# A two-block transformer kernel on one core: the opening rearranged (second row tile on ScalarE's DMA queue, first weight unit in two loads, row factors in fewer steps, meta tokens turned inside the first unit)

## The chip, the core and the metric

The kernel runs on one core of one Trainium2 chip. The core has a matrix engine (TensorE, PE in the rows), a vector engine (VectorE, DVE), an activation engine (ScalarE, ACT), a general engine (GpSimd, POOL) and a queue engine for transfers (SyncE, SP). ACT and POOL can issue transfers too. The five run their own instruction streams and meet at semaphores; each takes its instructions strictly in order, so one that waits holds up everything behind it on the same engine. The metric is the device time of one execution in microseconds (us). Matrices are float32, and each product is made from three passes over high and low parts, so weights are split before use: `whi` is the weight rounded to the matrix engine's format, `wlo` is the rest.

## The reference, cut to what matters

Two blocks follow each other on 256 rows of width 1024; 16 learned meta rows stand ahead of the real rows in the first block. What the change touches is only how the very first product is prepared:

```python
def rms_norm(x, g):
    xf = x.astype(jnp.float32)
    y = xf * lax.rsqrt(jnp.mean(xf * xf, axis=-1, keepdims=True) + RMS_EPS)
    return (y * g.astype(jnp.float32)).astype(x.dtype)

h = jnp.concatenate([filler, meta, x], axis=1)     # meta: 16 rows, x: 256 rows, width 1024
u = rms_norm(h, pre_mix_gain[l])
proj = u @ w_in[l]                                  # 1024 x 6656
# then: rope, windowed attention with meta keys, differential attention, gates,
# feed-forward, and the second block (delta rule, sparse attention, cross-attention,
# feed-forward); none of that is touched
```

## The kernel before

All weights stream through in units of 1 MB: a unit is 1024 rows by 256 columns (seen as 128 partitions x 8 x 256) or a shape of the same size. SP issues the loads into four buffers `raw`; ACT makes `whi` from `raw`, DVE makes `wlo`, each in halves (`split`), and PE multiplies. `plan` is a list of steps made by `schedule()`; each engine walks the same list and does its own part of each step, so the list fixes the order on every engine. The token `ahead` in the list lets the splits of coming halves stand early.

The opening before is this. SP loads row tile 0 of x, then row tile 1, then weight unit 0, a part of the constants (`ca`), unit 1 and so on; ACT issues the loads of the meta tokens (`metat`), of the identity matrix for transposes (`ca[:, 0:128]`) and of the gain columns (`pc[:, 0:8]`). The step `rows` computes for each of three row groups (tile 0, tile 1, meta) the sum of squares (ACT for tile 0 and meta, DVE for tile 1), the mean plus epsilon (DVE), the power -0.5 (POOL, `power`), and then the scaled rows `xs0` in halves of 512 columns: tile 0 and meta on DVE, tile 1 on ACT. The step `turn` transposes blocks of 128 columns by PE into PSUM and applies the gain: ACT writes the high part of the turned activations (`R1[0]`, "hi"), DVE the low part (`R1[1]`, "lo"). `turnm` does the same for the 16 meta rows, which become columns 256 to 271 of `R1`. The turned activations live in `R1b`.

Unit 0 is of the form `featk`: its split goes by halves of the contraction, so its first half (k-blocks 0 to 3) needs only lo 0 to 3 and the split (0, 0), and its second half needs lo 4 to 7 and (0, 1). It yields query columns, which the meta rows don't need. Unit 1 (keys) is the first that reads all 272 columns and so waits for the meta part, `norm_dve` key `("n1", "lo", 8)`.

Before PE's first real work it runs 13 matmuls on constants (`keep`), which depend on nothing but a memset.

## Time and profile before

| | |
|---|---|
| time, median of 3 runs | 960.5 us (960.37 to 960.55) |
| the profiled execution's own time | 960.5 us |
| its span, first to last instruction | 958.4 us |
| outside the span | 2.1 us |
| PE busy | 937.5 us, 98% |
| DVE, ACT, POOL busy | 674.6, 527.3, 137.9 us |
| granted TensorE clock, mean | 0.999 |
| first matmul of unit 0, of unit 1 | 12.82 us, 19.45 us |

Times inside the span are counted from its first instruction. Busy is the time in which an engine runs an instruction; waiting for a semaphore is not busy. A row of a timeline gives start, duration, engine, line, operation, what is written from what, and in brackets the idle time before it and who ended it. Successive instructions of one line and one pair of tiles are merged into one row with a count.

### The profile page before, as it was taken

What the parts mean: (1) busy time and instruction counts of PE and PEld (TensorE: products, weight loads), DVE (VectorE), ACT (ScalarE), POOL (GpSimd) and SP (SyncE); (2) the same over time, 40 slices, a digit from 0 to 9 for tenths busy, and PEclk for the clock granted to TensorE, in tenths of its full rate; (3) what the DMA queues carried; (4) which work ended last, traced back from release to release, by engine and by line L of the source; (5) the groups of instructions that cost most, each with busy time, mean ns of one, the idle gap of its engine ahead of it and who ended that gap; (6) DMA issues with size and microseconds to landing.
All of it is one profiled execution on the core that took longest, in us unless ns stands there. A gap on an engine that the chain in (4) does not pass through costs nothing.

```text
span 958.4 us, 15483 instructions
## 1 busy us (share of the span) xinstructions
PE 937.5 (98%) x6180; PEld 840.1 (88%) x6180; DVE 674.6 (70%) x1233; ACT 527.3 (55%) x1013; POOL 137.9 (14%) x159
## 2 busy tenths in 40 slices
PE   8999999999999999999999999899999999999996
PEld 7989888999999988888898899888798898888885
DVE  6888777777478676776758668767665567666765
ACT  6876665875456644444446686455454454344443
POOL 2211111220133000000001119941100000000001
PEclk9999999999999999999999999999999999999999
DMA  9544324343367555555565563300543455656441
GB/s 316 183 155 132 128 93 136 129 133 133 133 229 243 169 204 194 176 194 198 176 216 185 177 237 123 121 30 1 176 149 117 153 176 176 220 176 205 166 156 45
DMA packets 115863, 154.71 MB, mean 161 GB/s; under 512 B 2728, under 2 KB 98224, under 8 KB 115536
## 3 DMA queue, kind: packets, MB, share of 16 engines
q1 hardware_dynamic: 113376, 142.91, 44.9%
q0 software_dynamic: 1952, 10.42, 3.0%
q8 instruction: 49, 0.80, 0.4%
q10 hardware_dynamic: 464, 0.40, 0.2%
q14 instruction: 22, 0.18, 0.1%
HBM read 150.56 MB, written 3.16 MB: 160 GB/s over the span
## 4 chain that ended last, share of the span: by engine, by line
PE 89%; DVE 3%; POOL 3%; ACT 3%; issue 1%; DMA 0%; POOLq 0%; DVEq 0%; ACTq 0%
PE ps L847 14%; PE ps L823 8%; PE ps L825 8%; PE ps L824 8%; PE ps L848 7%; PE ps L1135 4%; PE ps L1108 4%; PE ps L1109 4%; PE ps L1110 4%; PE ps L866 4%; PE ps L868 4%; PE ps L867 4%; PE ps L809 3%; PE ps L836 2%; PE ps L838 2%; PE ps L837 2%
## 5 line engine op out<-in xcount | busy, mean ns | idle before, releaser
L1374 DVE TENSOR_TENSOR wlo<-raw,whi 128x1024 fp32r<-128x1024 f32 (+1 forms) x268 | 327.7, 1242 | 164.4 <-ACT whi L1986 164.0
L1986 ACT ACTIVATE whi<-raw 128x1024 fp32r<-128x1024 f32 (+1 forms) x268 | 273.8, 1050 | 129.9 <-PE ps L848 53.5
L847 PE MATMUL ps<-R1b,whi 128*128 128x512 f32 x576 | 201.8, 393 | 0.0
L823 PE MATMUL ps<-R1b,whi 128*128 128x256 f32 (+1 forms) x592 | 172.3, 291 | 0.8 <-DVE wlo L1374 0.8
L825 PE MATMUL ps<-R1b,wlo 128*128 128x256 f32 (+1 forms) x592 | 167.7, 283 | 0.0
L824 PE MATMUL ps<-R1b,whi 128*128 128x256 f32 (+1 forms) x592 | 167.5, 283 | 0.0
L848 PE MATMUL ps<-R1b,wlo 128*128 128x256 f32 x576 | 161.4, 280 | 0.0
L847 PEld LDWEIGHTS ps<-R1b,whi 128*128 128x128 f32 x576 | 108.1, 188 | 24.7 <-issue 0.5
L823 PEld LDWEIGHTS ps<-R1b,whi 128*128 128x128 f32 x592 | 111.6, 188 | 9.1 <-issue 7.9
L825 PEld LDWEIGHTS ps<-R1b,wlo 128*128 128x128 f32 x592 | 111.8, 189 | 0.0
L824 PEld LDWEIGHTS ps<-R1b,whi 128*128 128x128 f32 x592 | 111.5, 188 | 0.2
L848 PEld LDWEIGHTS ps<-R1b,wlo 128*128 128x128 f32 x576 | 108.2, 188 | 0.6
L2380 POOL TENSOR_TENSOR st<-st 128x1 f32<-128x1 f32 (+5 forms) x28 | 23.3, 838 | 375.4 <-DVE st L1367 299.8
L1108 PE MATMUL ps<-whi,R3ah 128*128 128x512 f32 x176 | 68.8, 391 | 0.0
L1109 PE MATMUL ps<-wlo,R3ah 128*128 128x512 f32 x176 | 68.8, 391 | 0.0
L1110 PE MATMUL ps<-whi,R3al 128*128 128x512 f32 x176 | 68.5, 389 | 0.0
L1986 ACT ACTIVATE F<-F 128x512 f32<-128x512 f32 (+6 forms) x58 | 28.9, 502 | 59.7 <-DVE F L1628 53.7
L1986 ACT ACTIVATE R3ah<-F 128x512 fp32r<-128x512 f32 x22 | 13.9, 632 | 68.1 <-DVE F L1650 68.1
L1617 DVE TENSOR_REDUCE F<-ps 128x256 f32<-128x512 f32 x72 | 49.3, 684 | 0.0
L1986 ACT ACTIVATE SC<-ps 128x512 f32<-128x512 f32 (+3 forms) x78 | 33.1, 429 | 21.0 <-PE ps L825 10.3
L1108 PEld LDWEIGHTS ps<-whi,R3ah 128*128 128x128 f32 x176 | 33.0, 188 | 7.2
L1110 PEld LDWEIGHTS ps<-whi,R3al 128*128 128x128 f32 x176 | 33.0, 188 | 7.2
(293 smaller groups left out, 1780.2 us busy)
## 6 DMA issues: line engine op xcount, KB each, us to landing
raw<-in_w_in SPq DMA_DIRECT2D x34, 1024.0 KB, 5.1
raw<-in_w_ffn_in SPq DMA_DIRECT2D x22, 1024.0 KB, 5.1
raw<-in_w_ffn_out SPq DMA_DIRECT2D x11, 1024.0 KB, 5.4
raw<-in_w_gate SPq DMA_DIRECT2D x11, 1024.0 KB, 5.3
raw<-in_w_up SPq DMA_DIRECT2D x11, 1024.0 KB, 5.3
raw<-in_w_down SPq DMA_DIRECT2D x11, 1024.0 KB, 6.0
raw<-in_w_out SPq DMA_DIRECT2D x8, 1024.0 KB, 5.1
raw<-in_w_xkv SPq DMA_DIRECT2D x8, 1024.0 KB, 5.5
```

What stands on the lines that cost most here:

```text
L823: e.matmul(o, hi[:, kt, c], R[0][:, kt, 0:n], start=kt == 0, stop=False)
L824: e.matmul(o, hi[:, kt, c], R[1][:, kt, 0:n], start=False, stop=False)
L825: m = e.matmul(o, lo[:, kt, c], R[0][:, kt, 0:n], start=False, stop=kt == 7)
L847: e.matmul(B[:, :].rearrange("p (a n) -> p a n", a=2), hi[:, kt, c], R[2][:, :, kt, 0:256], start=kt == 0, stop=False)
L848: m = e.matmul(B[:, 0:256], lo[:, kt, c], R[0][:, kt, 0:256], start=False, stop=kt == 7)
L866: e.matmul(B[:, 0:n], R[0][:, kt, c], hi[:, k, :], start=kt == 0, stop=False)
L1108: e.matmul(B[:, :], Fh[:, k, c], hi[:, k, d], start=j == 0 and k == 0, stop=False)
L1109: e.matmul(B[:, :], Fh[:, k, c], lo[:, k, d], start=False, stop=False)
L1110: m = e.matmul(B[:, :], Fl[:, k, c], hi[:, k, d], start=False, stop=end and k == 1)
L1374: e.tensor_tensor(half_of(wlo[i % HL], i, k), half_of(raw[i % RAW], i, k), f32(half_of(whi[i % HL], i, k)), SUB).then_inc(lo_split(i, (i, k)))
L1617: e.tensor_reduce(FSLOT[j % 2][0][:, at:at + 256], B[:, :].rearrange("p (a n) -> p n a", a=2), AX, ADD).then_inc(ffn_dve((kind, f, j, b)))
L1986: return e.activation(o, i, f, **kw)
```

## The change

Five edits, all in the opening:

1. Row tile 1 of x is loaded by ACT's queue, as its first transfer; the meta tokens become that queue's fourth and last.
2. Unit 0 of the weights is loaded in two transfers of 512 KB (k-blocks 0 to 3, then 4 to 7), with a semaphore of its own for the first.
3. Row factors: the mean plus epsilon is no longer a step of DVE. For tile 1 the DVE instruction that squares and sums takes the factor 1/1024 and starts from 1e-6; for tile 0 and meta POOL itself does that step ahead of its power. POOL runs one power on a constant before, at the start.
4. The scaling of tile 1's first half moves from ACT to DVE, that of the second half stays on ACT but stands behind the split (0, 0). Meta rows are scaled by POOL in one instruction of 16 x 1024.
5. The eight meta transposes of PE stand between the halves of unit 0; the gain step of DVE (`metax`) stands between lo 5 and lo 6, and the meta high and low parts (`metahl`) come behind the split (1, 0).

```diff
@@ schedule(): opening
         for j in range(2):
             take(0, j)
             step("ropek", j, 0)
+            if j == 0:
+                step("turnm")
-    step("rows", "n1")
+    step("first")
     ahead(1)
+    step("late")
     step("turn", "n1", (0, 2))
     ahead(2)
-    step("turn", "n1", (4, 6))
-    step("turnm")
+    step("turn", "n1", (4,))
+    step("metax")
+    step("turn", "n1", (6,))
+    ahead(3)
+    step("metahl")
@@ tensor: turnm
-                    p.wait_ge(norm_dve, ("n1", "sc", b // 4, 2))
+                    p.wait_ge(norm_pool, ("n1", "sc", 2))
@@ vector
+            def first():
+
+                v_, q = X[:, 1, :], stat(("n1", 1), 3)
+                d.wait_ge(*SOURCE["n1"][1])
+                ttr(xs0[1], v_, v_, 1.0 / 1024, 1e-6, MUL, ADD, q[:, 1:2]).then_inc(norm_dve(("n1", "ms", 1)))
+                for c, i in ((0, 0), (0, 1), (1, 0)):
+                    cs = slice(512 * c, 512 * c + 512)
+                    d.wait_ge(norm_pool, ("n1", "rs", i))
+                    ts(xs0[i][:, cs], X[:, i, cs], scale_of("n1", i)).then_inc(norm_dve(("n1", "sc", c, i)))
@@ scalar
             def split(i, k):
-                a.wait_ge(raw_in[i % RAW], i)
+                a.wait_ge(*((raw_first, 0) if (i, k) == (0, 0) else (raw_in[i % RAW], i)))
+            def first():
+                for i, (v_, m) in enumerate(rows_of("n1")):
+                    if i != 1:
+                        a.wait_ge(*SOURCE["n1"][i])
+                        act(xs0[i][0:m, :], v_, ACT.Square, accum_out=stat(("n1", i), 3)[0:m, 0:1]).then_inc(
+                            norm_act(("n1", "sq", i)))
+
+            def late():
+                a.wait_ge(norm_pool, ("n1", "rs", 1))
+                act(xs0[1][:, 512:1024], X[:, 1, 512:1024], scale=scale_of("n1", 1)).then_inc(norm_act(("n1", "sc", 1, 1)))
-            e.dma_start(metat, A["meta_tokens"]).then_inc(meta_in(0), 16)
+            e.dma_start(X[:, 1, :], A["x"].rearrange("a (t p) n -> p (a t) n", p=128)[:, 1, :]).then_inc(x1_in(0), 16)
             e.dma_start(ca[:, 0:128], A["const_a"][:, 0:128]).then_inc(id_in(0), 16)
             e.dma_start(pc[:, 0:8], A["params"][:, 0:8]).then_inc(mix_in(0), 16)
+            e.dma_start(metat, A["meta_tokens"]).then_inc(meta_in(0), 16)
@@ gpsimd
+            def first():
+                for i in (0, 1, 2):
+                    m = rows_of("n1")[i][1]
+                    q = stat(("n1", i), 3)[0:m]
+                    if i == 1:
+                        pool.wait_ge(norm_dve, ("n1", "ms", 1))
+                    else:
+                        pool.wait_ge(norm_act, ("n1", "sq", i))
+                        e.tensor_scalar(q[:, 1:2], q[:, 0:1], 1.0 / 1024, 1e-6, MUL, ADD).then_inc(norm_pool(("n1", "ms", i)))
+                        pool.wait_ge(norm_pool, ("n1", "ms", i))
+                    power(q[:, 2:3], q[:, 1:2]).then_inc(norm_pool(("n1", "rs", i)))
+                pool.wait_ge(norm_pool, ("n1", "rs", 2))
+                e.tensor_tensor(xs0[2][0:16, :], metat, scale_of("n1", 2).to_broadcast([16, 1024]), MUL).then_inc(
+                    norm_pool(("n1", "sc", 2)))
-            pool.wait_ge(set_dve, "half")
+            pool.wait_ge(set_dve, "one")
+            power(stat("warm", 1), ones).then_inc(set_pool("warm"))
@@ sync
-            e.dma_start(X[:, 1, :], x_src[:, 1, :]).then_inc(x1_in(0), 16)
...
+                dst = raw[i % RAW][:, 0:k * n].rearrange("p (k n) -> p k n", k=k)
+                if i == 0:
+                    e.dma_start(dst[:, 0:4, :], src[:, 0:4, :]).then_inc(raw_first(0), 16)
+                    src, dst = src[:, 4:8, :], dst[:, 4:8, :]
+                e.dma_start(dst, src).then_inc(raw_in[i % RAW](i), 16)
```

How the order stands on ACT from its first transfer to its first high parts of the turned activations, before; `in_x`, `in_meta`, `in_raw0` are the landings of row tile 0, of the meta tokens and of unit 0, and `in_raw_first` that of unit 0's first part:

```order
L2364 DMA F<-in_meta_tokens 16x1024
L2365 DMA ca<-in_const_a 128x128
L2366 DMA pc<-in_params 128x8
L1986 ACT_TABLE_LOAD
L1986 ACTIVATE F,st<-X 128x1024 [waits in_x]
L1986 ACTIVATE F,st<-F 16x1024 [waits in_meta]
L1986 ACTIVATE F<-X,st 128x512 [waits norm_pool]
L1986 ACTIVATE F<-X,st 128x512
L1986 ACTIVATE whi<-raw 128x1024 [waits in_raw0]
L1986 ACTIVATE R1b<-ps,pc 128x256 [waits norm_pe,in_mix]
```

And now, on the same engine:

```order
L2393 DMA X<-in_x 128x1024
L2394 DMA ca<-in_const_a 128x128
L2395 DMA pc<-in_params 128x8
L2396 DMA F<-in_meta_tokens 16x1024
L2004 ACT_TABLE_LOAD
L2004 ACTIVATE F,st<-X 128x1024 [waits in_x]
L2004 ACTIVATE F,st<-F 16x1024 [waits in_meta]
L2004 ACTIVATE whi<-raw 128x1024 [waits in_raw_first]
L2004 ACTIVATE F<-X,st 128x512 [waits norm_pool]
L2004 ACTIVATE R1b<-ps,pc 128x256 [waits norm_pe,in_mix]
```

The instruction that waits for the meta tokens still stands second, while their transfer has moved from the first place of the queue to the last; the first split has moved up by two places.

On POOL, from its last memset to its first work for rope, before and then now (`st` holds the row statistics, `F` the scaled rows):

```order
L2524 MEMSET F 128x1024
L2380 ISA
L2380 TENSOR_TENSOR st<-st 128x1 [waits norm_dve,set_dve]
L2380 TENSOR_TENSOR st<-st 128x1 [waits norm_dve]
L2380 TENSOR_TENSOR st<-st 16x1 [waits norm_dve]
L2392 TENSOR_TENSOR F<-SE 128x256 [waits rope_dve]
```

```order
L2569 MEMSET F 128x1024
L2410 ISA
L2410 TENSOR_TENSOR st<-st 128x1 [waits set_dve]
L2426 TENSOR_SCALAR st<-st 128x1 [waits norm_act]
L2410 TENSOR_TENSOR st<-st 128x1 [waits norm_pool]
L2410 TENSOR_TENSOR st<-st 128x1 [waits norm_dve]
L2426 TENSOR_SCALAR st<-st 16x1 [waits norm_act]
L2410 TENSOR_TENSOR st<-st 16x1 [waits norm_pool]
L2430 TENSOR_TENSOR F<-F,st 16x1024 [waits norm_pool]
L2437 TENSOR_TENSOR F<-SE 128x256 [waits rope_dve]
```

POOL has gained a power at the start, two steps of one column, and one product of 16 x 1024.

On DVE, from the first low part of the turned activations to the third split behind them, before and then now:

```order
L1374 TENSOR_TENSOR wlo<-raw,whi 128x1024 [waits hi_split]
L1364 SCALAR_TENSOR_TENSOR R1b<-ps,pc,R1b 128x256 [waits norm_act]
L1364 SCALAR_TENSOR_TENSOR R1b<-ps,pc,R1b 128x256
L1364 SCALAR_TENSOR_TENSOR R1b<-ps,pc,R1b 128x256 [waits norm_act]
L1364 SCALAR_TENSOR_TENSOR R1b<-ps,pc,R1b 128x256
L1431 TENSOR_TENSOR F<-ps,pc 128x128 [waits in_mix,norm_pe]
L1434 TENSOR_TENSOR R1b<-F,R1b 128x8x16 [waits norm_act]
L1374 TENSOR_TENSOR wlo<-raw,whi 128x8x128 [waits hi_split] x3
```

```order
L1380 TENSOR_TENSOR wlo<-raw,whi 128x1024 [waits hi_split]
L1370 SCALAR_TENSOR_TENSOR R1b<-ps,pc,R1b 128x256 [waits norm_act]
L1370 SCALAR_TENSOR_TENSOR R1b<-ps,pc,R1b 128x256
L1447 TENSOR_TENSOR F<-ps,pc 128x128 [waits in_mix,norm_pe]
L1370 SCALAR_TENSOR_TENSOR R1b<-ps,pc,R1b 128x256 [waits norm_act]
L1370 SCALAR_TENSOR_TENSOR R1b<-ps,pc,R1b 128x256
L1380 TENSOR_TENSOR wlo<-raw,whi 128x8x128 [waits hi_split]
L1452 TENSOR_TENSOR R1b<-F,R1b 128x8x16 [waits norm_act]
L1380 TENSOR_TENSOR wlo<-raw,whi 128x8x128 [waits hi_split] x2
```

The gain step of the meta tokens has moved up by two low parts, and the first split of unit 1 stands ahead of the meta tokens' low part instead of behind it.

## Rows read from the trace of the kernel before

**Rows 1.** The page, busy time, share of the span and instructions by engine.
```profile
PE 937.5 (98%) x6180; PEld 840.1 (88%) x6180; DVE 674.6 (70%) x1233; ACT 527.3 (55%) x1013; POOL 137.9 (14%) x159
```
**Rows 2.** Windows, PE alone: length, busy, matmuls, granted clock, DMA share, GB/s.
```profile
12.60:19.40 6.80, 5.87 (x48) 1.00 1.09 357
19.40:958.40 939.00, 921.52 (x6082) 1.00 0.48 158
```
**Rows 3.** Timeline of PE and its weight loads: start, duration, what.
```profile
11.30 0.57 PEld L809 LDWEIGHTS ps<-ca,F 16*128 16x128 f32 x8 [0.17 <-issue]
...
12.82 0.36 PE L947 MATMUL ps<-R1b,whi 128*128 128x256 f32 x1 [0.85 <-DVE R1b L1364]
...
19.45 0.36 PE L823 MATMUL ps<-R1b,whi 128*128 128x272 f32 x1 [0.75 <-DVE wlo L1374]
```
**Rows 4.** The chain of waits, 16.8 to 19.3 us.
```profile
16.79 0.31 ACT R1b L1986
17.10 0.96 ACT whi L1986
18.08 1.24 DVE wlo L1374
```
**Rows 5.** Timeline of ACT, first row tile to first high parts.
```profile
5.06 1.06 ACT L1986 ACTIVATE F<-X 128x1024 f32<-128x1024 f32 x1 [1.65 <-DMA X<-in_x]
...
6.11 1.04 ACT L1986 ACTIVATE F<-F 16x1024 f32<-16x1024 f32 x1
7.06 0.18 ACT L1986 ACTIVATION_READ_ACCUMULATOR F<-F 16x1 f32 x1
8.74 1.34 ACT L1986 ACTIVATE F<-X,st 128x512 f32<-128x512 f32 x2 [1.50 <-POOL st L2380]
9.98 1.04 ACT L1986 ACTIVATE whi<-raw 128x1024 fp32r<-128x1024 f32 x1
10.93 1.55 ACT L1986 ACTIVATE R1b<-ps,pc 128x256 fp32r<-128x256 f32 x4
```
**Rows 6.** Timeline of DVE, same stretch.
```profile
6.53 1.23 DVE L1370 CUSTOM_DVE_ANT_0 F<-X 128x1024 f32<-128x1024 f32 x1
...
8.19 0.49 DVE L1367 TENSOR_SCALAR F<-X,st 128x512 f32<-128x512 f32 x1 [0.19 <-POOL st L2380]
...
11.06 1.23 DVE L1374 TENSOR_TENSOR wlo<-raw,whi 128x1024 fp32r<-128x1024 f32 x1 [0.59 <-ACT whi L1986]
12.20 1.66 DVE L1364 SCALAR_TENSOR_TENSOR R1b<-ps,pc,R1b 128x256 fp32r<-128x256 f32 x4
```
**Rows 7.** Timeline of POOL: the powers of the row factors.
```profile
6.54 1.61 POOL L2380 TENSOR_TENSOR st<-st 128x1 f32<-128x1 f32 x1 [3.57 <-DVE st L1367]
...
8.12 1.04 POOL L2380 TENSOR_TENSOR st<-st 128x1 f32<-128x1 f32 x2
```
**Rows 8.** Timeline of POOL and DVE where they overlap, and POOL's widest products.
```profile
24.02 0.74 POOL L2392 TENSOR_TENSOR F<-SC,SD 128x256 f32<-128x256 f32 x1 [0.80 <-DVE SC L1458]
...
24.27 1.57 DVE L1374 TENSOR_TENSOR wlo<-raw,whi 128x1024 fp32r<-128x1024 f32 x1 [0.33 <-ACT whi L1986]
...
947.63 2.59 POOL L2517 TENSOR_TENSOR F<-X,F 128x512 f32<-128x512 f32 x2 [173.50 <-DVE X L1364]
```
**Rows 9.** DMA issues (0.73, 1.15, 1.62 us, ACT's 0.02 later): KB, us to landing.
```profile
X<-in_x SPq DMA_DIRECT2D x1, 512.0 KB, 4.3
F<-in_meta_tokens ACTq DMA_DIRECT2D x1, 64.0 KB, 3.5
...
X<-in_x SPq DMA_DIRECT2D x1, 512.0 KB, 5.4
...
raw<-in_w_in SPq DMA_DIRECT2D x1, 1024.0 KB, 8.0
ca<-in_const_a ACTq DMA_DIRECT2D x1, 64.0 KB, 5.6
pc<-in_params ACTq DMA_DIRECT2D x1, 4.0 KB, 6.1
```

More of the change, by code:

```diff
@@ L548, in program @@
         kv_out, kv_in = signal("kv_out", 16), signal("kv_in", 16)
-        raw_in = [signal(f"in_raw{i}", 16) for i in range(RAW)]
+        raw_first, raw_in = signal("in_raw_first", 16), [signal(f"in_raw{i}", 16) for i in range(RAW)]
         hi_split, lo_split = signal("hi_split"), signal("lo_split")
         gemm = signal("gemm")
-        set_dve, set_act = signal("set_dve"), signal("set_act")
+        set_dve, set_act, set_pool = signal("set_dve"), signal("set_act"), signal("set_pool")
         norm_pe, norm_act, norm_dve, norm_pool = [signal("norm_" + n) for n in ("pe", "act", "dve", "pool")]
@@ L887, in scaled @@
                 def scaled(i, b):
-                    p.wait_ge(norm_act if i == 1 else norm_dve, (s, "sc", b // 4, i))
+                    p.wait_ge(norm_act if i == 1 and (s != "n1" or b >= 4) else norm_dve, (s, "sc", b // 4, i))
                 if s in APART:
@@ L1426, in turn, with metax @@
                             f32(R[0][:, b + j, 0:256]), MUL, SUB).then_inc(norm_dve((s, "lo", b + j)))
-            def turnm():
+            def metax():
                 d.wait_ge(norm_pe, ("n1", "TX"))
@@ L1432, in turnm, with metahl @@
                                 par("pre_mix", 0, 8).unsqueeze(2).to_broadcast([128, 8, 16]), MUL).then_inc(norm_dve(("n1", "xv")))
+            def metahl():
                 d.wait_ge(norm_act, ("n1", "xhi"))
@@ L1974, in vector @@
             e.memset(ones, 1.0).then_inc(set_dve("one"))
-            parts = {"split": split, "rows": rows, "turn": turn, "turnx": turnx, "stat": stat_, "rsb": rsb_, "chunk": chunk, "chunk2": chunk2, "upg": upg, "setup": setup, "rotate": rotate, "turnm": turnm, "vt": vt, "swa": swa, "diff": diff,
+            parts = {"split": split, "rows": rows, "first": first, "turn": turn, "turnx": turnx, "stat": stat_, "rsb": rsb_, "chunk": chunk, "chunk2": chunk2, "upg": upg, "setup": setup, "rotate": rotate, "metax": metax, "metahl": metahl, "vt": vt, "swa": swa, "diff": diff,
                      "bsw": bsw, "bdf": bdf, "post": post, "upu": upu, "zc": zc, "tail": tail, "taps": taps, "zg": zg,
@@ L2027, in turn, with metahl @@
                             norm_act((s, "hi", b + j)))
-            def turnm():
+            def metahl():
                 a.wait_ge(norm_dve, ("n1", "xv"))
@@ L2362, in final @@
                     stored((1, 1)), 16)
-            e.dma_start(metat, A["meta_tokens"]).then_inc(meta_in(0), 16)
+            e.dma_start(X[:, 1, :], A["x"].rearrange("a (t p) n -> p (a t) n", p=128)[:, 1, :]).then_inc(x1_in(0), 16)
             e.dma_start(ca[:, 0:128], A["const_a"][:, 0:128]).then_inc(id_in(0), 16)
             e.dma_start(pc[:, 0:8], A["params"][:, 0:8]).then_inc(mix_in(0), 16)
-            parts = {"split": split, "rows": rows, "turn": turn, "turnx": turnx, "stat": stat_, "setup": setup, "rope": rope, "roped": roped, "turnm": turnm, "swap": swap, "v": v, "swa": swa,
+            e.dma_start(metat, A["meta_tokens"]).then_inc(meta_in(0), 16)
+            parts = {"split": split, "rows": rows, "turn": turn, "turnx": turnx, "stat": stat_, "setup": setup, "rope": rope, "roped": roped, "first": first, "late": late, "metahl": metahl, "swap": swap, "v": v, "swa": swa,
                      "diff": diff, "gate": gate, "merge": merge, "mem": mem, "psq": psq, "post": post, "upg": upg, "upu": upu, "conv": conv,
@@ L2524, in gpsimd @@
             e.memset(VB[:, 2, :], 0.0).then_inc(head_pool("zero"))
-            pool.wait_ge(set_dve, "half")
-            parts = {"rows": rows, "merge": merge, "rotate": rotate, "swa": swa, "diff": diff, "between": between, "post": post, "cbload": cbload, "smallload": smallload,
+            pool.wait_ge(set_dve, "one")
+            power(stat("warm", 1), ones).then_inc(set_pool("warm"))
+            parts = {"rows": rows, "first": first, "merge": merge, "rotate": rotate, "swa": swa, "diff": diff, "between": between, "post": post, "cbload": cbload, "smallload": smallload,
                      "kvout": kvout, "kvin": kvin, "taps": taps, "delta": delta, "dsa": dsa, "dsah": dsah, "stat": stat_, "g3load": g3load, "final": final}
@@ L2540, in sync @@
                     s.wait_ge(lo_split, i - RAW)
-                e.dma_start(raw[i % RAW][:, 0:k * n].rearrange("p (k n) -> p k n", k=k), src).then_inc(raw_in[i % RAW](i), 16)
+                dst = raw[i % RAW][:, 0:k * n].rearrange("p (k n) -> p k n", k=k)
[3 more added lines that the diff above has]
+                e.dma_start(dst, src).then_inc(raw_in[i % RAW](i), 16)
                 if i == 0:
```

## The prediction
> **What bounds the kernel now.** I read the page's first part first. PE is busy for 937.5 of 958.4 us [rows 1], so the question is where its 21 us of idle time lie and whether the change reaches them. The windows answer: from 19.40 us to the end PE is busy 921.5 of 939.0 us at full clock [rows 2], and the change touches nothing there. So PE sets the time from its unit 1 on, and what the change can give or take is how much earlier or later unit 1's first matmul starts; a shift there is handed to the end. It starts at 19.45 us, unit 0's at 12.82 [rows 3]. Unit 0's 48 matmuls take 5.87 us [rows 2], so PE is through at about 18.7 and waits 0.75 us for the split (1, 0).
>
> The chain of waits tells why: ACT made the meta tokens' high part at 16.79, only then the high part of unit 1's first half, and DVE its low part until 19.32 [rows 4]. The timelines of ACT and DVE tell what set 12.82: ACT was free for unit 0's first split only at 9.98, behind two scalings of tile 1 [rows 5]; DVE followed at 11.06, and only then at 12.20 came the first low parts [rows 6]. The first matmul came 0.62 after that.
>
> I sum against the profiled execution: 960.5 us, of which 958.4 is the span and 2.1 lie around it. That is also the median of the three runs, so the same difference applies to both.
>
> **Landings.** Before [rows 9], tile 0 landed at 0.73 + 4.3 = 5.03, tile 1 at 1.15 + 5.4 = 6.55, the meta tokens at 4.24, the identity at 6.77, the gain columns at 7.74, unit 0 at 9.62. Tile 1 came 1.5 us behind tile 0: that is the price of 512 KB. Now both tiles leave at once on two queues. Both together can't be there before 6.55 minus the share of the meta tokens and the identity (128 KB, 0.4): tile 1 at 6.1. Tile 0 lies between 5.03 (it is served first) and 6.1 (they alternate); I take 5.7. The first half of unit 0 needs half of the 3.1 us between 6.55 and 9.62: 8.1. Unit 1 and what is behind it have the same bytes ahead as before, cost nothing.
>
> The trace already has two such transfers side by side: tile 1 and the identity, issued 0.02 apart, landed at 6.55 and 6.77, and the identity took 5.6 us for 64 KB [rows 9]. The Trainium skill ("DMA: Bandwidth & Descriptors", Issuing engines are not separate DMA queues) says that transfers from different issuing engines run on the same sixteen engines and interleave, so that a second queue saves only issue time. By that rule edit 1 brings tile 1 forward by little and pushes tile 0 back; the trace agrees as far as it goes.
>
> The meta tokens move from first to last on ACT's queue. Tile 1 6.1; then the identity, for which the rows give 0.97 (what the gain columns took behind it) as a near neighbour and 2.5 (its own distance from the meta tokens, beside large rows) as a far one; I take 0.7, since it now runs beside unit 0 alone; gain columns 0.97; meta tokens 0.2: M = 8.0. Ends: 7.0 and 9.0. The identity and the gains land near where they did, before their users.
>
> **ACT and DVE up to the first matmul.** ACT squares tile 0 at 5.7 to 6.9 and then waits for the meta tokens; behind this wait stand the first split, tile 1's scaling and all high parts. From M = 8.0: the split starts 1.05 later (5.06 to 6.11 [rows 5]), 9.05; DVE's part 1.08 later (9.98 to 11.06 [rows 5, 6]), 10.13; it holds DVE to 11.27. On ACT the scaling follows at +0.95 (9.98 to 10.93), 10.0, takes 0.62 (half of 8.74 to 9.98), and two high parts of 0.39 (1.55 for four) end at 11.4. So the first low part starts at 11.4 and the first matmul 0.62 behind, at 12.0: 0.8 us earlier.
>
> The other path to that point is the row factors. Tile 1's squares on DVE run 6.1 to 7.35. POOL can't finish a power beside them: before, one that began at 6.54 took 1.61 and ended 0.4 behind DVE's 1.23 us instruction, the others 0.5 [rows 6, 7]. So POOL's step on tile 0, which no row shows (a power of one column is 0.5, so between 0.1 and 0.6; I take 0.3, below the power since it is simpler arithmetic), ends at 7.65, two powers at 8.9, two scalings on DVE by 9.8. That is below 10.13 and so hidden; it becomes the floor if M is early. The removed mean steps on DVE (two of 0.1 to 0.2 beside POOL's waiting) lie on this hidden path, and so does the early power: the 1.61 is explained by the overlap with DVE and not by a first use, so the early power is worth nothing and costs nothing, in POOL's idle time.
>
> **From there to unit 1.** PE needs 2.93 for half of unit 0, 0.57 for the eight meta transposes [rows 3], now in its stream, and 2.93: 12.0 + 6.45 = 18.45. DVE beside it: POOL's product of 16 x 1024 costs four times the slope of the 512-wide one (1.30 each [rows 8]), so 2.6 us. POOL and a DVE instruction with two such inputs exclude each other: a split of 1.23 beside a POOL product took 1.57, ending 1.1 behind it [rows 8]. The product starts when the first split ends, 11.3, ends 13.9, and holds up the split (0, 1), due at 13.0, to 15.0; PE wants it at 15.5, so this is covered with 0.5 to spare. Low parts 4 and 5 to 15.8, the meta gain step 0.3 (its transposes are done at 15.65), low parts 6 and 7 to 16.9, split (1, 0) to 18.0, meta low part to 18.3, unit 1 at 18.45. Both paths meet at the same time. The wait of 0.75 is gone, 0.57 of transposes has come in its place.
>
> Sum: -0.8 (first matmul), -0.75 (wait), +0.57 (transposes): -1.0. Span 957.4, time 959.5 us. Later splits on ACT wait for unit 0's end and shift by 0.25 less than PE; in the stretch from 19.40 nothing of them was last before PE by the windows, so I cost it at nothing; if that cover fails, 0.3.
>
> **Rivals.**
> - The meta tokens land at 8.7 or later. For it: three transfers ahead of them where there were none. Against it: 64 KB and 4 KB are little. Unit 1 starts at M + 10.45, so M = 9.0 gives exactly 19.45, no gain: 960.2 to 960.7. Chance 0.2.
> - The two tiles don't slow each other: tile 1 at 5.3, M = 7.2, unit 1 at 17.65, 1.8 earlier: 958.7, down to 958.2 if the small ones come along. For it: tile 0 and the meta tokens did overlap, and the moved bytes rise only slowly in the first microseconds. Against: 1.5 us for 512 KB. Chance 0.13.
> - POOL's product gets in before the first split of DVE, and takes the place of the removed waits. POOL has the meta sum at M + 1.13, then 0.15 of delay, step 0.3, power 0.55 and 0.2 between: M + 2.35, against M + 2.13 for the split. A margin of 0.2 decides. If POOL is first, the split ends at 10.3 + 2.6 + 1.1 = 13.9 and the first low part is 2.5 later than forecast: unit 1 at 20.9, 961.9 to 962.5, slower than before. For it: the exclusion works both ways in the rows. Chance 0.1. The Trainium skill ("GPSIMD Engine Reference", Specifications) names this: POOL's interfaces to the buffer are shared with VectorE, with contention where VectorE has two such inputs; the trace agrees with 1.57 in place of 1.23.
> - The shift is given back later, in one of the waits of the heads, so that the change does not show: 960.4. Against: those waits hang on PE's own products, and move along. Chance 0.07.
>
> **How the numbers follow.** The forecast has 0.5: 959.5, own range 958.9 to 960.1 (M from 7.4 to 8.6). A measurement of this kernel tells 0.2% (1.9 us) from no change. Faster than 958.6 needs the second rival at its far end: 0.12. Slower than 962.4 needs the third at its far end: 0.04. The rest, 0.84, is within. The range 958.4 to 961.0 takes in the first two rivals and the fourth, and leaves out most of the third.
>
> **What would show it.** Right: meta square on ACT about 8.0, first matmul of unit 0 at 12.0, eight transposes near 15, unit 1 at 18.4 without a wait on the split (1, 0), DVE's split (0, 1) stretched beyond 1.23. Wrong: ACT idle before the meta square until 9; a first split on DVE longer than 3 us; tile 0 landed at 5.0; a first power that still takes 1.6 with nothing of DVE beside it; or unit 1 earlier by 1 us and the end not.

## The result

The changed kernel takes 964.5 us (median of 6 runs, 963.77 to 965.33), the kernel before 960.5 in the same session; the ratio is 1.0036 with the interval [1.0023, 1.0049]. So it is slower by 4.0 us, where no measurable change was forecast (959.5, range 958.4 to 961.0). The profiled execution took 964.53 us with a span of 962.5. Executions of one kernel lie in groups 1 to 2 us apart, the longer ones with a lower mean granted clock (the kernel before: about 960.5 us with 0.998 and 962.0 with 0.996), and two single ones are left out of the ratios, 1324.17 us (one of 11 of the filled kernel with the product behind the split, clock 0.65) and 1031.39 us (the kernel before).

The page of the kernel after, span and busy time:

```profile
span 962.5 us, 15482 instructions
...
PE 941.1 (98%) x6180; PEld 843.1 (88%) x6180; DVE 675.6 (70%) x1229; ACT 526.9 (55%) x1012; POOL 139.8 (15%) x163
```

PE is busy 3.6 us longer than before [rows 1], with the same 6180 matmuls. The windows of the kernel after, PE alone (length, busy, matmuls, granted clock, DMA share, GB/s), cut at the changes of the granted clock and at unit 1's first matmul:

```profile
8.00:12.91 4.91, 3.01 (x22) 1.00 1.10 336
12.91:19.74 6.83, 5.14 (x25) 0.50 1.09 356
19.74:23.70 3.96, 3.96 (x36) 1.00 0.90 285
23.70:962.50 938.80, 921.94 (x6084) 1.00 0.47 157
```

From unit 1's first matmul on, 938.80 us pass; before it was 939.0 from 19.40 [rows 2]. So in the sum everything lost is lost ahead of 23.70 (two differences behind it cancel, see "What bounds the kernel" below). And in 6.83 us of that PE ran at a granted clock of 0.50, the 1.2 GHz level. Before, unit 0 ran at 1.00 [rows 2].

The PE timeline of the kernel after (start, duration, what, idle before):

```profile
12.25 1.17 PE L815 MATMUL ps<-ca,F 128*128 128x128 f32 x7 [1.90 <-ACT F L2004]
15.11 0.55 PE L953 MATMUL ps<-R1b,whi 128*128 128x256 f32 x1 [1.69 <-DVE R1b L1370]
...
16.11 0.41 PE L954 MATMUL ps<-R1b,whi 128*128 128x256 f32 x1
...
16.75 0.41 PE L954 MATMUL ps<-R1b,whi 128*128 128x256 f32 x1
...
20.19 0.66 PE L815 MATMUL ps<-ca,F 16*128 16x16 f32 x8
...
23.70 0.29 PE L829 MATMUL ps<-R1b,whi 128*128 128x272 f32 x1
```

Unit 0 begins at 15.11 instead of 12.82, unit 1 at 23.70 instead of 19.45 [rows 3]; the wait of 0.75 us in front of unit 1 is gone, and the eight transposes of the meta tokens (0.66) are in. The two L954 rows lie 0.64 us and three matmuls apart, 0.213 each; at full clock unit 0 took 5.87 us for 48, 0.122 each [rows 2]. From 15.11 to 19.74 that is some 22 matmuls by 0.091, 2.0 us lost to the clock.

What made unit 0 late? The chain of waits of the kernel after:

```profile
2.18 7.29 DMA F<-in_meta_tokens
...
10.64 0.95 ACT whi L2004
...
11.62 2.96 DVE wlo L1380
```

It starts with a transfer instead of an engine: the meta tokens. The DMA issues of the kernel after (KB, us to landing; SP's at 0.73, ACT's at 0.74, 1.17, 2.18 for the meta tokens and 1.65 for the gain columns):

```profile
X<-in_x SPq DMA_DIRECT2D x1, 512.0 KB, 5.1
X<-in_x ACTq DMA_DIRECT2D x1, 512.0 KB, 5.3
...
ca<-in_const_a ACTq DMA_DIRECT2D x1, 64.0 KB, 5.9
F<-in_meta_tokens ACTq DMA_DIRECT2D x1, 64.0 KB, 7.3
...
pc<-in_params ACTq DMA_DIRECT2D x1, 4.0 KB, 7.2
```

ACT's timeline of the kernel after:

```profile
9.49 1.06 ACT L2004 ACTIVATE F<-F 16x1024 f32<-16x1024 f32 x1 [2.50 <-DMA F<-in_meta_tokens]
...
10.55 1.04 ACT L2004 ACTIVATE whi<-raw 128x1024 fp32r<-128x1024 f32 x1
```

POOL's, its last power and its product:

```profile
10.99 0.54 POOL L2410 TENSOR_TENSOR st<-st 16x1 f32<-16x1 f32 x1
11.60 1.89 POOL L2430 TENSOR_TENSOR F<-F,st 16x1024 f32<-16x1024 f32 x1
```

And DVE's, the first split and the first low parts:

```profile
11.62 2.96 DVE L1380 TENSOR_TENSOR wlo<-raw,whi 128x1024 fp32r<-128x1024 f32 x1 [2.14 <-ACT whi L2004]
14.50 1.65 DVE L1370 SCALAR_TENSOR_TENSOR R1b<-ps,pc,R1b 128x256 fp32r<-128x256 f32 x4
```

ACT squares tile 0 as soon as it has landed (0.73 + 5.1), then stands for 2.50 us until the meta tokens are there, and squares them at 9.49. The first split follows at 10.55 (before 9.98 [rows 5]). POOL has the meta tokens' row factor and starts its product at 11.60, DVE its split at 11.62. The split's row is 2.96 us long where it was 1.23 [rows 6]: it ends 1.09 us behind the product. Only then comes the first low part, at 14.50 in place of 12.20.

### The profile page after: what moved, and what is told of

Its sections match the earlier page's. It is cut to its first block, busy times and chain, and to the rows that moved or that the text cites. A ratio compares the mean times of both kernels' runs of the same rounds, so it can differ in the third digit from the quotient of the medians.

```text
span 962.5 us, 15482 instructions
## 1 busy us (share of the span) xinstructions
PE 941.1 (98%) x6180; PEld 843.1 (88%) x6180; DVE 675.6 (70%) x1229; ACT 526.9 (55%) x1012; POOL 139.8 (15%) x163
## 4 chain that ended last, share of the span: by engine, by line
PE 89%; DVE 3%; POOL 3%; ACT 3%; issue 1%; DMA 1%; ACTq 0%; POOLq 0%; DVEq 0%
PE ps L853 14%; PE ps L829 8%; PE ps L831 8%; PE ps L830 8%; PE ps L854 7%; PE ps L1141 4%; PE ps L1114 4%; PE ps L1115 4%; PE ps L1116 4%; PE ps L872 4%; PE ps L874 4%; PE ps L873 4%; PE ps L815 3%; PE ps L842 2%; PE ps L844 2%; PE ps L843 2%
```

## The experiments

All were made from the changed kernel unless said otherwise, and timed beside the kernel before. "First matmul" is that of unit 0, in the profiled execution. The theory: three costs one behind the other, (a) the meta tokens land late, (b) POOL's product gets ahead of DVE's first split and holds it, (c) PE idles in front of unit 0, the granted clock falls, and unit 0 runs at half speed.

**Edit 1 undone** (tile 1 second on SP's queue, meta tokens first on ACT's):

```diff
 # ACT
-e.dma_start(X[:, 1, :], ...).then_inc(x1_in(0), 16)
+e.dma_start(metat, A["meta_tokens"]).then_inc(meta_in(0), 16)
...
-e.dma_start(metat, A["meta_tokens"]).then_inc(meta_in(0), 16)
 # SP, behind tile 0
+e.dma_start(X[:, 1, :], x_src[:, 1, :]).then_inc(x1_in(0), 16)
```

> The changed kernel with the first edit undone: row tile 1 second on SyncE's queue, meta tokens first on ScalarE's; the other four edits stay, GpSimd's product free to stand ahead of the split. Theory A: tile 0 at 5.0, meta square at 6.1, tile 1 at 6.5, scalings on VectorE done at 9.7, its first split at 9.7, GpSimd's product ready at 9.8: if the split is first, first matmul at 11.4, unit 1 at 17.9 and 958.9; if the product is first, 960.5. Rival B (the other edits cost too): above 960.5 even with a short first split.

Measured: 958.98 us (958.66 to 960.59), ratio 0.9986 [0.9976, 0.9995]. ACT's timeline of this kernel, the meta tokens' squares:

```profile
6.01 1.04 ACT L2004 ACTIVATE F<-F 16x1024 f32<-16x1024 f32 x1
```

DVE's, the first split:

```profile
9.44 1.22 DVE L1380 TENSOR_TENSOR wlo<-raw,whi 128x1024 fp32r<-128x1024 f32 x1
```

PE's window from unit 0 to unit 1:

```profile
11.34:17.85 6.51, 6.51 (x57) 1.00 1.09 357
```

The meta tokens' squares stand at 6.01, the first split on DVE at 9.44 with 1.22 us, the first matmul at 11.34, the clock is full: as expected. POOL's product starts at 10.00 here, 0.56 behind the split, and now it is POOL's row that is long, 2.41 us in place of 1.89. Without edit 1 the rest of the change is worth 1.5 us, and edit 1 costs it 5.5. Unit 1 starts 1.60 us earlier than in the kernel before; 0.8 of it is lost behind that point, and a last store that lands 0.9 sooner hides the loss (see "What bounds the kernel" below).

**Edit 1 alone**, on the kernel before:

```diff
 # kernel before, ACT
-e.dma_start(metat, A["meta_tokens"]).then_inc(meta_in(0), 16)
+e.dma_start(X[:, 1, :], ...).then_inc(x1_in(0), 16)
...
 e.dma_start(pc[:, 0:8], ...)
+e.dma_start(metat, A["meta_tokens"]).then_inc(meta_in(0), 16)
 # SP
-e.dma_start(X[:, 1, :], x_src[:, 1, :]).then_inc(x1_in(0), 16)
```

> The kernel before with the first edit alone: row tile 1 by ScalarE's queue, the meta tokens last on it. Theory A (the late meta tokens hold ScalarE): meta square at 9.4, behind it two scalings and the first split at 11.8 instead of 9.98, first matmul 14.6 instead of 12.82; time 962.3, and 2 more where TensorE's clock is halved. Rival (the tokens' place on the queue costs nothing, since ScalarE would wait for weights anyway): 960.4.

Measured: 964.08 us, with runs from 961.27 to 966.11, ratio 1.0031 [1.0019, 1.0043]. ACT's timeline of this kernel:

```profile
9.00 1.05 ACT L1986 ACTIVATE F<-F 16x1024 f32<-16x1024 f32 x1 [2.15 <-DMA F<-in_meta_tokens]
```

And the window of PE in which the granted clock was half:

```profile
11.56:18.39 6.83, 6.83 (x36) 0.50 1.09 357
```

The squares of the meta tokens wait 2.15 us here too, until 9.00, and the half clock covers 11.56 to 18.39. PE stands for 2.17 us, since DVE's mean step for the meta tokens comes only at 10.18 and the scalings stand behind it. There is no product on POOL in this kernel, so (a) and (c) alone make it slower. The first matmul comes at 14.94 (expected 14.6). The mean granted clocks tell (a) and (c) apart: with 0.997 to 0.998 three executions took 961.3 to 961.8 us, with 0.996 one took 962.67, and with 0.994 six took 964.0 to 966.1. So the late tokens cost about 1 us where the clock seems to have been kept, and the rest goes with the clock.

**Meta tokens first, tile 1 second, both on ACT's queue:**

```diff
+e.dma_start(metat, A["meta_tokens"]).then_inc(meta_in(0), 16)
 e.dma_start(X[:, 1, :], ...).then_inc(x1_in(0), 16)
...
-e.dma_start(metat, A["meta_tokens"]).then_inc(meta_in(0), 16)
```

> The meta tokens are again the first transfer of ScalarE's queue, tile 1 of x the second; nothing else. Theory A: the meta square starts behind tile 0's, near 6.9 instead of 9.49, the first split of ScalarE near 8.1, when its half unit has landed. GpSimd's product then comes ready about 0.1 us from the split again, so the split is either 1.2 or near 3 us long: first matmul at 11.5 or near 13; time 960.5 or lower if the product loses the race, 961 to 962 if it wins. Rival B (the order on the queue does not matter, both tiles and the small transfers interleave anyway): meta square still after 9 us and the time at 964.5.

Measured: 959.57 us (959.07 to 961.17), ratio 0.9989 [0.9979, 0.9998]; first matmul 12.03, granted clock 1.00 throughout unit 0. DVE's timeline:

```profile
7.27 1.23 DVE L1376 CUSTOM_DVE_ANT_0 F<-X 128x1024 f32<-128x1024 f32 x1 [6.38 <-DMA X<-in_x]
...
10.13 1.22 DVE L1380 TENSOR_TENSOR wlo<-raw,whi 128x1024 fp32r<-128x1024 f32 x1
```

Tile 1 landed only at 7.27, behind the meta tokens and beside tile 0, which landed at 5.02 as before. So the second queue brought tile 1 nothing here: it was there at 6.53 on SP's queue [rows 6]. What the order of the queue gives back is 4.9 us. The expected race was not seen, for the row factors of the late tile 1 held POOL up too: its product started at 10.69, 0.56 behind the split, and took 2.41 us.

**Product behind the first split:**

```diff
 pool.wait_ge(norm_pool, ("n1", "rs", 2))
+pool.wait_ge(lo_split, (0, 0))
 e.tensor_tensor(xs0[2][0:16, :], metat, ...)
```

> GpSimd's product of the meta rows waits for the low part of split (0, 0) as well; nothing else. Theory A (the changed kernel loses at three places: 0.6 us because ScalarE waits for the meta tokens, 1.7 us because GpSimd's product stands in front of VectorE's first split, 2.1 us because TensorE then idles and its clock is halved over unit 0): the first split takes 1.23 us instead of 2.96, the first matmul of unit 0 comes at 13.4 instead of 15.11, and the time falls by 1.7 us, by 3.8 if the shorter idle time keeps the clock up. Rival B (the split was long for another reason, for instance a read of weights that were still landing): the split stays near 3 us and the time at 964.5. Rival C (the clock falls whatever the idle time): 1.7 us gained, clock still half over some of unit 0.

Measured: 960.48 us (960.39 to 964.0), ratio 1.0002 [0.9992, 1.0012]. DVE's timeline of this kernel, the first split:

```profile
11.21 1.23 DVE L1380 TENSOR_TENSOR wlo<-raw,whi 128x1024 fp32r<-128x1024 f32 x1 [1.97 <-ACT whi L2004]
```

POOL's, the product:

```profile
12.58 1.89 POOL L2431 TENSOR_TENSOR F<-F,st 16x1024 f32<-16x1024 f32 x1 [1.47 <-DVE wlo L1380]
```

PE's window at half clock:

```profile
11.84:15.26 3.42, 3.42 (x16) 0.50 1.08 366
```

The split takes 1.23 us again, and the next one, now beside the product, 1.36. The first matmul is at 13.24, 1.87 earlier, of which 0.41 come from the meta tokens' landing (9.08), which differs from run to run. Unit 1 is 3.00 earlier: the rest is the half clock, now 3.42 us long and not 6.83. The single wait gives back 4.0 us in the median and 3.0 in the profiled execution (961.5), which is not a typical one: it has a mean granted clock of 0.997, while six others with 0.998 to 0.999 took 960.39 to 960.48.

**Both**, the order of the queue and the wait:

```diff
+e.dma_start(metat, A["meta_tokens"]).then_inc(meta_in(0), 16)
 e.dma_start(X[:, 1, :], ...).then_inc(x1_in(0), 16)
...
-e.dma_start(metat, A["meta_tokens"]).then_inc(meta_in(0), 16)
...
+pool.wait_ge(lo_split, (0, 0))
```

> Meta tokens first on the queue and the product behind the first split. Theory A: first split of ScalarE near 8.1, of VectorE near 9.8 and 1.23 long, first matmul near 11.4, unit 1 near 17.9, no halved clock: 959.0, 1.5 us below the kernel before. Rival B (there is a cost elsewhere in the change, such as tile 0 landing 0.8 us later, that no order of the meta tokens removes): 960.5 or more.

Measured: 959.87 us (959.17 to 961.43), ratio 0.9992 [0.9982, 1.0001], no better than with the queue's order alone: there POOL's product (10.69) came behind the split (10.13) anyway. The expected 959.0 was missed by 0.9: tile 1 lands late here too (7.10), and the first matmul comes at 11.86 and not 11.4.

**PE filled** in its two gaps ahead of unit 0 with matmuls whose result nobody reads (each of the four is recorded as two matmuls in the trace):

```diff
 step("turn", "n1", (0, 2))
+step("more", 4)
...
 step("metahl")
+step("more", 4)
```

> Eight more matmuls on constants for TensorE, four behind the first two transposed pairs and four ahead of unit 0, where it idles in the changed kernel; everything else as changed, the late meta tokens and the product ahead of the split included. Theory A: the clock stays at full over unit 0, whose first half takes 2.9 us instead of 4.7; the first matmul stays near 15.1 (up to 0.3 later); time 962.4, that is 2.1 less. Rival C (the clock falls for another reason than idle time): half clock stays over part of unit 0 and the time at 964.5.

Measured: 962.2 us (961.71 to 963.65), ratio 1.0018 [1.0009, 1.0028]. PE's windows:

```profile
8.00:14.90 6.90, 6.74 (x39) 1.00 1.08 351
14.90:21.40 6.50, 6.50 (x56) 1.00 1.10 348
...
678.36:681.78 3.42, 3.17 (x10) 0.50 0.92 383
```

PE's timeline ahead of the last of these:

```profile
676.40 0.63 PE L817 MATMUL ps<-ca,F 128*128 128x128 f32 x4 [1.23 <-DVE F L1375]
...
678.61 1.19 PE L1320 MATMUL ps<-F,SD 128*128 128x256 f32 x2 [0.92 <-DVE st L1901]
```

The split is as long as in the changed kernel (2.95 us at 11.40) and the first matmul as late (14.90), but PE is busy 6.74 of the 6.90 us ahead of it, and unit 0 runs at 1.00: 6.50 us instead of 8.59 to unit 1. That is (c) by itself, 2.1 us in the trace and 2.3 in the time. This profiled execution lost the clock once more, at 678.36 us, in no connection with the start, between waits of PE of 1.23 and 0.92 us; it took 963.65 us, and six others 961.7 to 962.3. The kernel before has the same two waits there (1.24 and 0.92) and kept the clock in its profiled execution. A late fall of this size, 1.5 us in the time, would also fit the difference between 960.5 and 962.0 us of the kernel before; only this one is in a trace.

**Filled, and the product behind the split:**

```diff
+pool.wait_ge(lo_split, (0, 0))
...
+step("more", 4)
...
+step("more", 4)
```

> Changed kernel with POOL's product behind the first split, and with four more matmuls that go nowhere on TensorE in each of its two idle gaps ahead of unit 0. Theory (three separate costs: the late landing, the held split, the clock): first matmul of unit 0 at 13.0 to 13.2, granted clock full over unit 0, unit 1 at 19.8, 959.8 to 960.2 us. Rival (the two last costs are one: without the held split the filling buys nothing): as the kernel with the product behind the split alone, 960.5.

Measured: 961.95 us (961.58 to 963.59, and the one of 1324.17), ratio 1.0013 [1.0004, 1.0023]. Both expectations missed: it is slower than the product behind the split alone. PE's timeline:

```profile
12.60 1.91 PE L822 MATMUL ps<-st 128*128 128x256 f32 x8
14.15 0.47 PE L955 MATMUL ps<-R1b,whi 128*128 128x256 f32 x1
```

The clock is full, but the second filling runs from 12.60 to 14.15 and beyond what PE would have waited for: without it the first matmul was at 13.24. The filling costs 0.9 us and unit 0 gains 0.84 (6.62 us against 7.46), so unit 1 starts at 20.77 against 20.70. That compares two profiled executions, with spans of 959.6 and 959.5 us. The medians lie 1.5 us apart, for the profiled one of the unfilled kernel is not typical, as said above. If the clock did not fall in its six others with 0.998 to 0.999, unit 1 starts at some 13.24 + 6.62 = 19.86, and with 938.8 behind it the span is 958.7; the spans of these six are 958.3 to 958.4. So there was most likely nothing there for the filling to give back, and its 0.9 us and more are pure cost. For those six only the mean of the clock is on record, not its course.

**Product with one input** (the factor as a column, not spread as a second tensor):

```diff
-e.tensor_tensor(xs0[2][0:16, :], metat, scale_of("n1", 2).to_broadcast([16, 1024]), MUL)
+e.tensor_scalar(xs0[2][0:16, :], metat, scale_of("n1", 2), None, MUL)
```

> The changed kernel with GpSimd's product of 16 x 1024 written with one tensor input and a column factor instead of two tensor inputs; its place and everything else as changed. Theory A1 (the two engines exclude each other only where both read two tensors): VectorE's first split takes about 1.3 us though GpSimd runs beside it, first matmul near 13.4, time 962.8 or, with the clock kept, 960.7. Theory A2 (any GpSimd instruction of that width holds VectorE's split up): the split stays near 3 us or longer, first matmul 15.1, time 964.5.

Measured: 960.46 us (959.9 to 962.16), ratio 0.9997 [0.9988, 1.0006]. POOL's timeline of this kernel, the product:

```profile
10.88 3.94 POOL L2430 TENSOR_SCALAR F<-F,st 16x1024 f32<-16x1024 f32 x1
```

DVE's, the first and the second split:

```profile
10.87 1.23 DVE L1380 TENSOR_TENSOR wlo<-raw,whi 128x1024 fp32r<-128x1024 f32 x1 [1.67 <-ACT whi L2004]
...
13.86 1.23 DVE L1380 TENSOR_TENSOR wlo<-raw,whi 128x1024 fp32r<-128x1024 f32 x1
```

The time and the kept clock are as theory A1 had them, but that does not confirm it. The meta tokens landed earlier in this execution (8.74), and DVE was first by 0.01 us, so it doesn't tell who would have held whom. The next split at 13.86 does lie beside POOL's instruction, which ends at 14.82, and is not held. So two more runs put the start of the product beyond doubt.

**Product well ahead, two inputs.** Edit 1 is undone, and the meta tokens' squares and factor come first:

```diff
 # ACT
-for i, (v_, m) in enumerate(rows_of("n1")):
+for i in (2, 0):
 # POOL
-for i in (0, 1, 2):
+for i in (2, 0, 1):
```

> Changed kernel with edit 1 undone (tile 1 second on SP's queue, meta tokens first on ACT's), and the meta tokens' squares and row factor taken ahead of tile 0's, so that POOL's product (two tensor inputs, 16 x 1024) starts at about 8.75 us, well ahead of the first split on DVE, which is ready at about 9.57. Theory (a POOL product with two inputs holds back a DVE split for as long as it runs, and DVE then runs the split in full): product 8.75 to 10.65, the split's row 9.57 with 2.3 us, first matmul of unit 0 at 12.7, one more us idle on PE, 959.5 us at full clock and some 2 us more if the clock falls. Rival (the split was long in the changed kernel for another cause, such as late data or its two halves): split row 1.23 us, first matmul at 11.6, 958.4.

Measured: 961.45 us (960.16 to 961.85), ratio 1.0003 [0.9994, 1.0012]. POOL's timeline of this kernel, the product:

```profile
8.95 1.88 POOL L2429 TENSOR_TENSOR F<-F,st 16x1024 f32<-16x1024 f32 x1
```

DVE's scalings of X in the view of one tile (least, median and greatest ns, first and last start):

```profile
L1373 DVE TENSOR_SCALAR F<-X,st x3: 475/485/2036, 8.5 to 11.0; 128x512 f32<-128x512 f32 x3
```

DVE's timeline, the split:

```profile
11.44 1.21 DVE L1380 TENSOR_TENSOR wlo<-raw,whi 128x1024 fp32r<-128x1024 f32 x1
```

The theory's price was right, and its victim wrong. The instruction caught was the scaling in front of the split, which has one tensor input: 2036 ns in place of 485, from 9.08 to 11.12, 0.3 behind the product's end. The split then ran in 1.21. The Trainium skill ("SBUF — State Buffer", Who interferes with whom) says that the port pair VectorE and GpSimd share is an exclusive lock for the whole instruction, taken by whichever starts first, and that a tensor_scalar in a two-port mode wants it as much as an instruction with two inputs. The trace agrees, with 2.04 us. PE then waited 1.72 us for that scaling, and the granted clock was 0.50 from 11.09 to 14.50, so that the 15 transposes behind it took 3.46 us instead of 1.86 (edit 1 undone): the first matmul came at 14.29, 1.6 later than the theory's 12.7. Seven executions, the profiled one among them, took 961.4 to 961.9 us with a mean clock of 0.997, the other four 960.2 to 960.6 with 0.998 to 0.999; the theory had 959.5 at full clock.

**Product well ahead, one input**, again with edit 1 undone:

```diff
 # ACT
-for i, (v_, m) in enumerate(rows_of("n1")):
+for i in (2, 0):
 # POOL
-for i in (0, 1, 2):
+for i in (2, 0, 1):
...
-e.tensor_tensor(xs0[2][0:16, :], metat, scale_of("n1", 2).to_broadcast([16, 1024]), MUL)
+e.tensor_scalar(xs0[2][0:16, :], metat, scale_of("n1", 2), None, MUL)
```

> The same, but the product is a TENSOR_SCALAR (one tensor input and a column of factors). Theory: it starts at 8.75 and runs for 3.9 us, across the whole of the first split, and doesn't hold it: split row at 9.57 with 1.23 us, first matmul of unit 0 at 11.7, 958.4 to 958.7 us. Rival (any POOL work on a wide tile holds the split): split row of 4 us, first matmul at 14, 961 us or more.

Measured: 959.63 us (959.52 to 961.38), ratio 0.9988 [0.9979, 0.9996], first matmul 12.39, full clock. POOL's timeline of this kernel, the product:

```profile
8.79 2.85 POOL L2429 TENSOR_SCALAR F<-F,st 16x1024 f32<-16x1024 f32 x1
```

The view of the tile, DVE's scalings:

```profile
L1373 DVE TENSOR_SCALAR F<-X,st x3: 474/486/1276, 8.3 to 10.1; 128x512 f32<-128x512 f32 x3
```

DVE's timeline, the split:

```profile
10.50 1.21 DVE L1380 TENSOR_TENSOR wlo<-raw,whi 128x1024 fp32r<-128x1024 f32 x1
```

The split lies beside the product for 1.14 us and takes 1.21: not held, which is the part of the theory that mattered. But the time is 1 us above the expected 958.4 to 958.7, for a scaling was held: it started at 8.90, 0.11 behind the product, and took 1276 ns in place of 486. If it ran its 486 ns in one piece at the end, it was held for 0.79 us, until 9.69. That fits a POOL instruction that holds DVE for its first 0.9 us and not for its whole 2.85, and the rule of the Trainium skill ("SBUF — State Buffer", Who interferes with whom) of the whole instruction doesn't; one run is too little to call it shown.

**The meta tokens first of all:** edit 1 undone, ACT squares and scales them itself, POOL has no product, and their transposes stand ahead of unit 0:

```diff
 # ACT
-for i, (v_, m) in enumerate(rows_of("n1")):
+for i in (2, 0):
...
+a.wait_ge(norm_pool, ("n1", "rs", 2))
+act(xs0[2][0:16, :], metat, scale=scale_of("n1", 2)).then_inc(norm_act(("n1", "sc", 2)))
 # POOL
-for i in (0, 1, 2):
+for i in (2, 0, 1):
...
-e.tensor_tensor(xs0[2][0:16, :], metat, ...)
 # schedule()
 step("turn", "n1", (0, 2))
+step("turnm")
...
-if j == 0:
-    step("turnm")
```

> First edit undone, and the meta tokens' whole chain taken ahead: ScalarE squares them before tile 0 and scales them itself while it waits for weights, GpSimd makes their factor first and no product at all, TensorE turns them behind the first two pairs, where it idles, not between the halves of unit 0. Theory A: first split of ScalarE near 8.2, of VectorE near 9.7 and 1.23 long, first matmul near 11.4, unit 0 without the 0.6 of transposes, unit 1 near 17.3; 958.3, 2.2 below the kernel before and 6.2 below the changed one. Rival (VectorE's chain of low parts and splits binds unit 1 once the transposes are gone): unit 1 near 17.8, 958.8.

Measured: 958.4 us (958.06 to 960.06, 9 runs), ratio 0.9979 [0.9969, 0.9988], as expected (958.3) and the best of all, 2.1 us below the kernel before and 6.1 below the changed one. ACT's timeline of this kernel:

```profile
4.23 1.05 ACT L2003 ACTIVATE F<-F 16x1024 f32<-16x1024 f32 x1 [0.82 <-DMA F<-in_meta_tokens]
...
5.28 1.04 ACT L2003 ACTIVATE F<-X 128x1024 f32<-128x1024 f32 x1
...
6.38 1.15 ACT L2003 ACTIVATE F<-F,st 16x1024 f32<-16x1024 f32 x1
```

PE's windows ahead of unit 0 and over it:

```profile
8.00:11.67 3.67, 3.37 (x29) 1.00 1.09 359
11.67:17.39 5.72, 5.72 (x52) 1.00 1.09 359
```

ACT's wait for tile 0 covers the squares, and its wait for unit 0 the scaling (1.15 us); unit 0 takes 5.72 us without the transposes inside, and PE is busy 3.37 of 3.67 us ahead of it.

## Why the prediction was wrong

Three steps failed: the meta tokens' landing (M = 8.0, measured 9.49), the race between POOL's product and the first split (held to be lost by the product by 0.2 us, won by 0.02, at a price of 1.68 us), and the unasked clock, taken as full over unit 0 (0.50 over most of its first half, 2.14 us). In the prediction's own order:

- **What bounds the kernel.** Right among the kernels made from the changed one: a shift of unit 1 is handed to the end. From there 938.75 to 938.85 us were left in the changed kernel and in nine of the ten others; the tenth is the filled kernel (940.31, with the late fall of the clock). That the kernel before comes out the same (938.9) is luck: two differences cancel. Matmul by matmul, PE falls back against the kernel before by 0.5 us at the 25th of unit 1 and by 0.8 within 17 us. The 25th waits for ACT's copies out of PSUM:

```profile
27.25 0.36 PE L829 MATMUL ps<-R1b,whi 128*128 128x272 f32 x1 [0.37 <-ACT SC L2004]
```

The kernel before has no wait there (22.54); its pause of 0.75 us in front of unit 1 had covered it. This is the cover that the prediction took for granted ("I cost it at nothing; if that cover fails, 0.3"). It failed, and cost 0.8 and not 0.3: the fourth rival, in part. In return the last store landed sooner. The last transfers of the kernel before, and then of the changed one:

```profile
out<-F ACTq DMA_DIRECT2D x1, 256.0 KB, 3.5
```

```profile
out<-F ACTq DMA_DIRECT2D x1, 256.0 KB, 2.6
```

It is 2.6 us in every kernel made from the changed one. Edit 1 alone has the first difference and not the second (3.5 us), hence its 939.76. Why the store takes 3.5 us in those two is open; a packet of an instruction queue lies in the last 12 us of both and of no other. Every gain against the kernel before, the 1.5 and the 2.1 us too, has both in it, the 0.8 lost and the 0.9 of the store.
- **Landings.** Tile 0 at 5.84 (forecast 5.7), tile 1 at 6.04 (6.1), the first half of unit 0 at 7.95 (8.1): right. The identity landed at 7.07 (6.8), the gain columns at 8.85 (7.8). M, the meta tokens, 9.49, beyond the end of 9.0 given for it. The steps that failed are the small ones: 0.97 for the gain columns came out as 1.78, 0.2 for the meta tokens as 0.63, and the identity came 0.3 late. The rows said how small transfers fare beside 512 KB ones; unit 0's transfers were beside them now too, and they were treated as nearly free. M was 8.74 to 9.49 in the six kernels with the meta tokens last on ACT's queue. Rival 1 came true.
- **First split.** M + 1.05 on ACT and M + 2.13 on DVE: measured 10.55 and 11.62, exact.
- **POOL's product.** Rival 3 came true as well, with its margin of 0.2: 11.60 against 11.62. Its mechanism is shown by the product behind the split, and the other way round by the two kernels in which the product started 0.56 behind the split and took 2.41 us (edit 1 undone, meta tokens first). Its start was forecast at M + 2.35 and came at M + 2.11, because the step (0.18) and the gaps were smaller than estimated. The product was sized at 2.6 and measured 1.89. The chance of 0.1 was far too low for a race decided by 0.2 us, of which the terms were known to 0.3.
- **First matmul.** Forecast 12.0, measured 15.11: 1.49 from M, and 1.68 from the held split (14.57 for its end, against 11.4 + 1.49 for what would else have been last).
- **Unit 0 to unit 1.** Forecast 6.45, measured 8.59. The transposes are as forecast (0.57, measured 0.66), the wait of 0.75 is gone. The 2.1 left are the granted clock, which the prediction did not look at: it read "at full clock" as a given. It considered rivals that make PE wait, and did not ask what PE does after it has waited. The filled kernel shows it.
- **Early power.** Right: the very first power, with nothing of DVE beside it, took 0.53 us at 3.02, so there is no price of a first use. The powers for tile 0 and tile 1 took 1.12 for two. With edit 1 undone the one beside DVE's squares took 1.58 in spite of the early power, as the 1.61 before [rows 7].
- **Sum.** 1.49 + 1.68 + 2.14 = 5.3 against 5.25 measured (23.70 for unit 1, 18.45 forecast), and 5.0 in the time. The rest of the change, without edit 1, started unit 1 1.6 us earlier than before and gained 1.5 in the time.
- **The rivals were priced one at a time.** Rival 1 gave 960.7, rival 3 962.5 and both together by the same sums 22.4 for unit 1. The sum had no term for both at once, though nothing keeps them apart: a late M delays the product and the split by the same amount, so the race stays as close as it was. The last 1.3 us (23.70 against 22.4) are the clock's 2.1 less 0.9, by which the held split ended sooner than estimated: the product began 0.2 earlier and was 0.7 shorter.
- **Edit 1 itself.** The argument was that tile 1 arrives 0.45 earlier; it did (6.04 against 6.55), and that moved nothing, for the path to the first matmul ran over the meta tokens. The Trainium skill ("DMA: Bandwidth & Descriptors", Issuing engines are not separate DMA queues) had it that queues of two engines interleave and save issue time only; the prediction quoted that, and the trace agrees with 5.03 to 5.84 for tile 0. The cost lay in what stood behind on the same queue.

## What to carry to other kernels

When a transfer is put at the head of a queue, price the one that lands last on it by measured small transfers beside the same traffic, and see which engine waits for it in program order: 64 KB at the end of ACT's queue instead of at its head cost 4.9 us here. An instruction of POOL that reads the buffer should be ordered by a wait behind the VectorE instruction that is on the path, since a margin of 0.02 us decided 1.7 us. And after each forecast of an idle stretch on TensorE ask for the granted clock behind it; if it may fall, the stretch costs more than its length. When the time behind a mark comes out equal in two kernels, compare the rows behind it all the same: here 0.8 us lost and 0.9 gained hid each other.

## What the runs showed of the hardware

- The granted clock fell to 0.50 with gaps of 1.72 to 2.17 us on PE ahead of unit 0 (the changed kernel 1.90, edit 1 alone 2.17, product behind the split 1.85, product well ahead 1.72), and not where the longest gap ahead of unit 0 was 0.53 us (meta tokens first), 0.85 (the kernel before), 0.96 (product well ahead, one input) or 0.97 (product with one input). The fall cost 2.1 us over unit 0 in the changed kernel and 0.84 with the product behind the split, 1.4 with edit 1 alone (7.27 us against 5.87), and 1.6 over the transposes with the product well ahead. In one execution it also fell at 678 us, between gaps of 1.23 and 0.92 us, which cost that one 1.5 us; the same gaps stand in traces without a fall. So the length of a gap alone does not decide, and what does stays open.
- A POOL product of 16 x 1024 with two inputs takes 1.89 us, and 2.85 us as a tensor_scalar with one input (3.94 when it starts together with a DVE split). The slower form is the better neighbour: 959.6 against 961.5 us, the clock that fell beside the other included, and against 960.2 to 960.6 in the executions that seem to have kept it.
- A scaling on DVE of 0.49 us was held by POOL's product to 2.04, as a split is (1.23 to 2.96). A start 0.02 us ahead decides who is held; where DVE's split started 0.56 ahead, POOL's product took 2.41 us in place of 1.89.
- The same last store of 256 KB took 3.5 us from issue to landing in two kernels and 2.6 in eleven, with the same neighbours; why is not shown.
